# Job buffers, the place of the row columns and the shape of the key and value weights in the first stage of a three-block forward pass

## The reference, cut to what matters

```python
m = silu(c) @ ev_mod_w + ev_mod_b            # 2048 x 6144 weights; also for c_ctx
shift, scale, gate = m[..., :D], m[..., D:2*D], m[..., 2*D:]
h  = rmsnorm(x,   pre_g) * (1 + scale)   + shift      # 512 tokens
hc = rmsnorm(ctx, pre_g) * (1 + scale_c) + shift_c    # 256 tokens
proj = h @ w_in                              # queries, keys and values, gate z
kA, vA, kB, vB = split_kv(proj[..., 2048:3072])
kA_c, vA_c, kB_c, vB_c = split_kv(hc @ w_in[:, 2048:3072])
```

## Time and profile before

| | us |
|---|---|
| median of 3 runs | 2537.2 |
| lowest and highest | 2536.16, 2540.18 |
| the profiled execution | 2535.82 |
| its span | 2534.0 |
| PE busy in the span | 2497.7 (99%) |
| DVE busy | 1623.8 (64%) |
| ACT busy | 973.6 (38%) |

### The profile page before, as it was taken

The page is one execution under the profiler, slowest core; times in us unless marked ns, Lnnn a source line. Parts: engine busy times, 40 slices in busy tenths (PEclk is TensorE's granted clock), DMA queues, the critical chain, the costliest instruction groups (busy, mean ns, idle before and its releaser), DMA issues.

```text
span 2534.0 us, 30108 instructions
## 1 busy us (share of the span) xinstructions
PE 2497.7 (99%) x11975; PEld 2020.2 (80%) x11975; DVE 1623.8 (64%) x2444; ACT 973.6 (38%) x1549; POOL 110.7 (4%) x117
## 2 busy tenths in 40 slices
PE   7999999999999999999999999999999999999999
PEld 4789777777777887888888887888888787887887
DVE  4456776677776768776776768456365577656532
ACT  4232444444444333432434333445455432333421
POOL 0000000000000114000000113000000000000000
PEclk8999999999999999999999999999999999999999
DMA  9955433434433754666645754323222245532342
GB/s 350 336 193 185 127 110 121 125 125 133 132 101 136 258 180 157 208 200 211 200 162 175 249 175 158 111 76 91 80 87 84 75 151 169 175 112 89 123 154 83
DMA packets 293133, 390.58 MB, mean 154 GB/s; under 512 B 11698, under 2 KB 221234, under 8 KB 289154
## 3 DMA queue, kind: packets, MB, share of 16 engines
q1 hardware_dynamic: 287184, 355.84, 43.5%
q0 software_dynamic: 5808, 32.84, 3.5%
q10 hardware_dynamic: 2, 0.00, 0.0%
HBM read 371.85 MB, written 16.78 MB: 153 GB/s over the span
## 4 chain that ended last, share of the span: by engine, by line
PE 89%; DVE 5%; DMA 2%; ACT 2%; issue 1%; SPq 1%; POOL 0%; DVEq 0%; ACTq 0%; POOLq 0%
PE G L2151 74%; PE OB L2151 6%; PE S L2151 6%; PE TB L2154 2%; PE TB L2151 1%; DMA MRAW<-in_ev_mod_w 1%; DMA MORE<-in_ev_mod_w 1%; DVE WLO L1634 1%; DVE MACC L1640 1%; DVE TT L1634 1%; ACT PB L1445 1%; DVE SM L1862 0%; SPq L1129 0%; PE OB L2154 0%; DVE Y L1634 0%
## 5 line engine op out<-in xcount | busy, mean ns | idle before, releaser
L2151 PE MATMUL G<-HHI,WLO 128*128 128x512 f32 x2560 | 1001.0, 391 | 0.0
L2151 PE MATMUL G<-HHI,WHI 128*128 128x512 f32 x1964 | 801.8, 411 | 0.5 <-DVE CLO L1640 0.5
L2151 PE MATMUL G<-HLO,WHI 128*128 128x512 f32 x1928 | 753.2, 391 | 1.6 <-DVE HLO L1640 1.4
L2151 PEld LDWEIGHTS G<-HHI,WLO 128*128 128x128 f32 x2560 | 480.7, 188 | 104.3
L1272 ACT ACTIVATE WHI<-RAW 128x1024 fp32r<-128x1024 f32 x282 | 297.5, 1056 | 560.9 <-PE G L2151 501.6
L1634 DVE TENSOR_TENSOR WLO<-RAW,WHI 128x1024 fp32r<-128x1024 f32 x282 | 344.5, 1222 | 234.9 <-ACT WHI L1272 233.0
L2151 PEld LDWEIGHTS G<-HHI,WHI 128*128 128x128 f32 x1964 | 370.9, 189 | 80.3 <-issue 6.7
L2151 PEld LDWEIGHTS G<-HLO,WHI 128*128 128x128 f32 x1928 | 363.1, 188 | 79.7 <-issue 6.7
L1640 DVE SCALAR_TENSOR_TENSOR MACC<-MWIDE,SC,MACC 128x512 f32<-128x512 f32 x420 | 320.4, 763 | 39.2 <-DMA MWIDE<-in_w_ada 12.8
L2151 PE MATMUL G<-HHI,WHITA 128*128 128x512 f32 x536 | 215.0, 401 | 0.0
L2151 PE MATMUL G<-HLO,WHITA 128*128 128x512 f32 x536 | 209.2, 390 | 0.0
(11 more groups left out here) (347 smaller groups left out, 3060.7 us busy)
## 6 DMA issues: line engine op xcount, KB each, us to landing
RAW<-in_w_in SPq DMA_DIRECT2D x128, 512.0 KB, 3.7
MWIDE<-in_od_mod_w SPq DMA_DIRECT2D x96, 512.0 KB, 4.1
MWIDE<-in_w_ada SPq DMA_DIRECT2D x96, 512.0 KB, 4.6
RAW<-in_ev_w_in SPq DMA_DIRECT2D x80, 512.0 KB, 3.5
RAW<-in_od_w_in SPq DMA_DIRECT2D x64, 512.0 KB, 3.9
MWIDE<-in_ev_mod_w SPq DMA_DIRECT2D x32, 512.0 KB, 3.8
RAW<-in_ev_w_out SPq DMA_DIRECT2D x32, 512.0 KB, 3.3
RAW<-in_od_w_out SPq DMA_DIRECT2D x32, 512.0 KB, 3.3
```

Source lines behind the costliest of these rows:

```text
L2151: return e.o.matmul(o, l, r, start=start, stop=stop, skip_group_check=True)
```

## The change

Four things change together.

1. **Columns and tiles of h.** `row_cols` is put two jobs behind the row's last job, as before, but for row 1 directly behind its last job; `h_pair` stands with it. The pieces of the pair go to `ready` two jobs later, where they stood back for a row (four jobs) before. Behind the jobs 1 and 2 pieces are taken in turn, where it was 0, 2, 0, 3.
2. **Ten buffers.** Two buffers (EXTRA) are new. A job takes the buffer that has been free longest; each LATE buffer is used until its part of HLO comes due.
3. **Weights by two k tiles.** The 8 transfers of key and value weights hold two k tiles by 512 columns, keys and values together. A buffer is given back after two k tiles. The first transfer is put behind job 1 as before, which is now behind the transfers of jobs 10 and 11; the second behind job 4 (before: 3), the third to fifth behind job 7, and the sixth, which waits for its buffer, behind job 9; the first two splits are put behind job 7 and with the first pair of h.
4. **Room.** The memory set aside for POOL's DMA descriptors is given as 8192 bytes.

Two of the four spills move: they stand behind jobs 59, 61 and twice 63. Widths of 512 columns for a row are provided for in the code but not used (`WIDTHS` holds eight times 256).

```diff
-    job_slot = ([i % 8 for i in range(32)] + [(0, 1, 2, 3, 6, 7)[i % 6] for i in range(18)]
-                + [(0, 1, 2, 3)[i % 4] for i in range(14)])
...
+    rings = MRAW + MORE + LATE + EXTRA
+    free_from = {4 + x: row_end[row_of_pair[4 + x]] - 3 for x in range(4)}
...
+        slot = min((x for x in range(10) if i <= free_from.get(x, i)), key=lambda x: last_in.get(x, x - 10))
...
         def prologue():
-            for i in range(8):
+            for i in range(10):
                 put("job_load", i)
...
                 put("job_row", i)
-                if i + 8 < len(jobs0):
-                    put("job_load", i + 8)
-                if i in (1, 3, 5):
+                if i in job_behind:
+                    put("job_load", job_behind[i])
+                if i in (1, 4, 9):
                     load_next()
-                if c == 3:
+                if i == row_end[n]:
                     put("row_copy", n)
+                    later.setdefault(i if n == 1 else i + 2, []).append(n)
...
-                if i in (9, 11, 13):
+                if i == row_end[1]:
                     split_next()
                     loads()
-                if c == 1 and n > 0:
-                    put("row_cols", n - 1)
-                    ready += near
-                    near = []
-                    if n % 2 == 0:
-                        put("h_pair", n // 2 - 1)
-                        near = pieces(n // 2 - 1)
-                if i > 51 and i % 4 == 3:
-                    put("x_spill", i // 4 - 13, i)
-                for _ in range((0, 2, 0, 3)[i % 4]):
+                for m in later.pop(i, ()):
+                    put("row_cols", m)
+                    for pair in row_pairs[m]:
+                        put("h_pair", pair)
+                        if m == 1 and pair < 2:
+                            split_next()
+                        later.setdefault(("near", i + 2 + 2 * (pair - row_pairs[m][0])), []).append(pair)
+                for pair in later.pop(("near", i), ()):
+                    ready += pieces(pair)
+                if i in (59, 61):
+                    put("x_spill", (i - 59) // 2, i)
+                for _ in range((1, 2)[i % 2]):
                     if ready:
                         kv_piece(*ready.pop(0))
...
-            if k % 4 == 3 and part == (1 if what == "k" else 2):
+            if k % 2 == 1 and what == "v" and part == 2:
                 used(at["done"])
                 split_next()
...
-    nc = bacc.Bacc("TRN2", target_bir_lowering=False, num_devices=1)
+    nc = bacc.Bacc("TRN2", target_bir_lowering=False, num_devices=1, dynamic_dma_scratch_size=8192)
```

More of the change, by code:

```diff
@@ L116, in build @@
         MWIDE.append(place(f"MWIDE{i}", [P, 2, 512], F32, at)[0])
+    EXTRA = [place(f"EXTRA{i}", [P, 4, 256], F32)[0] for i in range(2)]
     MACC, _ = place("MACC", [P, 512], F32)
@@ L210, in build @@
     raw = [sig(f"raw{i}") for i in range(NR)]
-    mraw = [sig(f"mraw{i}") for i in range(8)]
+    mraw = [sig(f"mraw{i}") for i in range(10)]
     par, sel, cst, rope, tri, spill, rcd, dkd = map(sig, ("par", "sel", "cst", "rope", "tri", "spill", "rc", "dk"))
@@ L264, in build @@
     ev_w, od_w, w2 = T["ev_w_in"][0], T["od_w_in"][0], T["w_in_2"][0]
-    def both(w, n0, n1):
-        return [c for two in zip(weight(w, n0), weight(w, n1)) for c in two]
     def three(w, *cols):
         return [c for each in zip(*[weight(w, n) for n in cols]) for c in each]
-    units = [both(ev_w, 2048, 2304), weight(ev_w, 2560), weight(ev_w, 2816)]
+    units = [weight_512(ev_w, 2048), weight(ev_w, 2560), weight(ev_w, 2816)]
     for p in range(8):
@@ L595, in prologue @@
             put("x_rstd")
-            ready, near = [], []
-            for i, (nb, c) in enumerate(jobs0):
-                n = i // 4
+            ready = []
+            later = {}
+            for i, (n, c) in enumerate(jobs0):
                 put("job_row", i)
-                if i + 8 < len(jobs0):
-                    put("job_load", i + 8)
-                if i in (1, 3, 5):
+                if i in job_behind:
+                    put("job_load", job_behind[i])
+                if i in (1, 4, 9):
@@ L621, in prologue @@
+                for pair in later.pop(("near", i), ()):
[3 more added lines that the diff above has]
+                for _ in range((1, 2)[i % 2]):
                     if ready:
                         kv_piece(*ready.pop(0))
[L623 to L626, removed]
+            for at_job in sorted(j for j in later if isinstance(j, int)):
+                for m in later[at_job]:
+                    put("row_cols", m)
+                    for pair in row_pairs[m]:
+                        put("h_pair", pair)
@@ L627, in prologue @@
+            for q in (2, 3):
+                put("x_spill", q, 63)
+            for pair in sorted(p for j, pairs in later.items() if not isinstance(j, int) for p in pairs):
+                ready += pieces(pair)
+            for piece in ready + pieces(7):
                 kv_piece(*piece)
@@ L1127, in sp_program @@
                     e.wait_ge(p_row, job_before[i])
-                nb, c = jobs0[i]
-                e.o.dma_start(rings[slot][:, :, :], weight(T["ev_mod_w"][0], 256 * nb)[c]).then_inc(
-                    *mraw[slot].up(("job", i), by=16))
+                n, c = jobs0[i]
+                width, c0 = rows0[n]
+                if width == 512:
+                    tile, src = shaped(rings[slot], 2), wide(T["ev_mod_w"][0], c0 // 512, c)
+                else:
+                    tile, src = rings[slot][:, :, :], weight(T["ev_mod_w"][0], c0)[c]
+                e.o.dma_start(tile, src).then_inc(*mraw[slot].up(("job", i), by=16))
             elif stage == "load":
@@ L2228, in pe_program @@
                 k, what, part = a
-                i = k // 4 * 2 + (0 if what == "k" else 1)
-                wh, wl, j = whi(i), WLO[i % NR], k % 4
+                i, j = k // 2, k % 2
+                wh, wl = shaped(whi(i), 2), shaped(WLO[i % NR], 2)
                 hi, lo = HHI[:, k, :], HLO[:, k, :]
@@ L2251, in pe_program @@
                         vh, vl = (HHI[:, k, cols], HLO[:, k, cols]) if part < 2 else (CHI[:, k, cols], CLO[:, k, cols])
[L2252 to L2255, removed]
-                if last and j == 3:
-                    t.then_inc(*p_gemm.up(i, *([(0, 1 if what == "k" else "v")] if end else [])))
+                        mm(o, vh, wh[:, j, wv], begin and x == 0, False)
+                        mm(o, vl, wh[:, j, wv], False, False)
+                        t = mm(o, vh, wl[:, j, wv], False, end)
+                if what == "k" and part == 1 and end:
+                    t.then_inc(*p_gemm.up((0, 1)))
+                elif what == "v" and part == 2 and j == 1:
+                    t.then_inc(*p_gemm.up(i, *([(0, "v")] if end else [])))
             elif stage == "mm":
```

65 lines of the change are left out of this document (42 added, 23 removed).

## The result

The changed kernel takes 2580.05 us (median of 4 runs, 2574.67 to 2581.29), the kernel before 2537.28 beside it. The ratio is 1.0163, 95% interval [1.0147, 1.0178]: 43 us slower, 1.6%. The profiled execution took 2580.07 us with a span of 2578.3, 44.3 more than the span before. The forecast was 2572 in a range of 2553 to 2586.

The account below looks back on a forecast made before the run. TensorE, busy 99% of the span, was taken as the bound. Start 1.1, moved work 1.9, groups 6.8 and net waits 18.8 gave 28.6; with clock 7.0, 35.6 on 2535.8, plus 1.4 to the median: 2572 us, range 2553 to 2586.

Parts of the forecast that it names:

- the chain (part 1): Columns' transposes to a pair's first piece: 5.16 us, 2.09 covered in steady pairs; seven TensorE waits for CLO, 22.7 us.
- the start (parts 2 and 3): First weights land 3.0 us later; first piece at about 47.65, 1.1 us later; jobs and columns moved behind it 1.9.
- the groups: First stage on TensorE: 22 more groups of jobs at 0.31 us each cost 6.8 us, bounds 0 and 12.5.
- the clock: TensorE's clock can fall at each new gap; four of seven taken, 7.0 us, ends 0 and 12.3.
- 35.6: Predicted total loss in us: 28.6 for start, moved work, groups and net waits, plus the clock's 7.0.
- two falls: Clock falls read in the kernel before: 1.7 us lost around 1535 us, and 1.9 at the start.
- The rival with a fall at every wait (2578): TensorE's clock falls at all seven waits: 28.6 + 12.3 = 40.9, 2578 us; inside the forecast's 0.78, no own chance.
- SP held (parts 2 and 3): SP held at the sixth weight transfer until 62.7 us; job 20 has 8.5 us left; cost 0, at most 3.
- part 4: POOL's list and the moved spills: last two land at 173, keys done at 177; cost 0, at most 8.
- The chain is not covered (2550): Denies the rival that the chain is largely covered: about 10 of waits and 3 of start, 2550 us; chance 0.11.
- POOL is not held (2580): Denies the rival that POOL is held, 8 us more, 2580; POOL or SP held beyond the forecast: 0.04.
- the transfers do not set the pace: Denies the rival that transfers pace the first stage and new waits only replace others: 6.9 us faster, 2530.3; chance 0.07.

Follow-up runs that it names:

- The held pieces: The changed kernel with a pair's pieces released four jobs behind its columns instead of two: 2548.75 us, ratio 1.0043.
- the good order: Changed kernel with pieces released four jobs behind columns, jobs in pairs, no weight load behind job 9: 2540.00 us; with first weight transfer behind job 7's, 2534.84.
- The run with the earlier weights: The changed kernel with its first key and value weight transfer right behind job 7's: 2573.21 us, ratio 1.0139.
- the fastest kernel: Changed kernel, pieces released four jobs behind columns, jobs in pairs, no weight load behind job 9, first weight transfer behind job 7's: 2534.84 us, ratio 0.9990.
- eight buffers: The 2534.84 us kernel with eight job buffers instead of ten: 2539.33 us, ratio 1.0005.

## Why the prediction was right, and where it was not

**Right: the chain (part 1).** Seven waits of 22.7 us were predicted and seven of 22.7 us were measured: 4.04 for the first (3.8), 3.07 for pairs 2 to 6 (3.07), 3.36 for the last (3.5). The chain of 5.16 us read at the end of the old stage is the same everywhere. The held pieces show it from the other side: cover it with two more jobs and their pieces, and of the seven waits only the 0.5 at the last pair is left.

**Right: the start (parts 2 and 3).** First piece at 47.75, predicted 47.65. Moving the first weight transfer four places ahead, behind eight jobs' transfers instead of twelve, moves the first piece by 5.0 us in the changed kernel and by 5.9 in the good order; at 1.5 us for each transfer that is 6.

**Nearly right: the groups.** A lone job takes from 98.24 to 100.06 with a key piece of 1.05, so 0.77, which is 0.34 beyond the job's 0.43; the prediction had 0.31. The period of a pair without a fall is 17.73 us (17.6 predicted). Putting jobs back into pairs gave 4.6 us for 19 groups fewer (44 and 25), 5.6 with the longer wait for CLO added back, 0.30 for each.

**Mis-sized: the clock.** The step that failed is "I take four of seven, 4 x 1.75 = 7.0 us". It fell at six, and each cost 2.6: 15.7 us. With that, 35.6 - 7.0 + 15.7 = 44.3, and the stage grew by 44.8. Both factors were wrong. The 1.75 was read from two falls. The run with the earlier weights shows falls of two sizes, 1.5 and 2.6 us. The fall at 1535 is of the small one. That at the start had begun at 40 us, while TensorE still waited for jobs' data, and only its tail was charged. The count was a guess, since no row had such a gap; of the stretches of 3.7 us that the prediction names, the rows show one. The upper end, 7 x 1.75 = 12.3, did not hold the true 15.7. The marker that belonged to it, the next unit's first product at 182 to 190, was missed as well: it came at 198.07. The rival with a fall at every wait (2578) came nearer than the forecast.

The Trainium skill, "TensorE: Matmul & The Clock Gate", section "Why this matters for your kernels", warns of long idle gaps between bursts. The trace agrees at six of seven gaps, with 3.06 to 4.04 us of wait. It did not hold at each: the gap with 3.36 us at 189.49, and one with 3.07 in the run with the earlier weights, kept 1.00. The prediction said that its two falls agree with the page. Only the one at the start lies behind waits (2.01 and 0.87 us); ahead of the other TensorE was idle for 0.25 us.

**Right for its reason, but with luck: SP held (parts 2 and 3).** Costed at 0, at most 3. In the changed kernel no job waits for it. With the chain covered it costs 4.57 us and a fall. SP issued the transfer at 62.78 (62.7 predicted), and job 20, due at 71.2 by the prediction, started at 73.27; the slack was the waits' own, so the 0 held only as long as the loss did.

**Right: part 4.** No wait behind the stage changed by more than 0.3 us. The descriptor memory by itself is 1.0001 on the kernel before, and no run shows it holding POOL back.

**The rivals.** The chain is not covered (2550), POOL is not held (2580), and the transfers do not set the pace: their waits went to nothing. The DMA engines run without a pause until 125 us only in the fastest kernel, where the waits for CLO are removed and the weights come earlier, and that one is 2.8 us ahead of before, not the rival's 6.9.

**What stays open.** What decides between a fall of 2.6, one of 1.5 and none behind the same 3.07 us. The pattern moved when everything was shifted by 5 us, so the moment at which a gap comes seems to play a part; no run isolates it. The gap at 189.49, the one that kept the clock, is also the only one with no jobs right ahead of it; but in the run with the earlier weights the same gap let the clock fall, for 1.5 us. The changed kernel's own 6.6 us of spread between runs would fit with it, but only one execution of it is traced. Why eight buffers are slower than ten in most runs is not settled, and the wait for ROW was not removed by any run.

## What to carry to other kernels

When an order is rewritten so that a result is used as soon as it can be there, measure the chain behind it once, where the engine really waits for it, and count what is left to lie over it; the chain of 5.16 us less what lay over it gave the sum of the seven waits to the tenth of a us. A gap of some 3 us of idle time on TensorE must be priced as itself and up to 2.6 us of halved clock behind it, here 15.7 on top of 22.7. And a wait that goes uncovers the next: behind CLO stood job 20's transfer, and behind that the copy of a row.

## What the hardware showed that was not expected

- The same idle gap of 3.07 us let TensorE's clock fall for a price of 2.6 us, of 1.5 us or not at all in one run, and waits of 2.36 us, each with two jobs before it, lost it behind three of five.
- 5.39 us of products of 32 columns and nothing else kept the granted clock at 1.00, as full products do. In the kernel before, 3.7 us of products of one column and transposes, with 0.25 us of idle time, did not.
- 40 such products (float32 on both sides, four parts of the array in turn) took 4.3 us, 0.11 each, where 24 products of 128 columns and the same width, with operands rounded to fp32r, took 3.13, 0.13 each. A product with a quarter of the columns was hardly cheaper.
